# Two-layer trunk kernel: the second pair of heads projected between the first norms, side products spread anew, the gating norm by logarithm and exponential

## The reference

```python
h = rmsnorm(x, norm_mix_g[l]);  proj = h @ w_in[l]          # 1024 -> 5384 columns
logf = log_sigmoid(proj[F] + b_forget[l])                   # 8 forget gates
zc = gelu(proj[C]);  gates = sigmoid(proj[G] + b_gate[l])
y_a = pool_mixer(a, pool_w, pool_scale) @ w_branch_a        # means over 2, 4, 8, 16 positions
y_b = forgetting_attention(q, k, v, logf) @ w_branch_b      # 8 heads of 64, causal, bias F[t]-F[s]
y_c = spatial_gating(zc, sgu_norm_g, sgu_w, sgu_b) @ w_branch_c
x = x + (gates_a * y_a + gates_b * y_b + gates_c * y_c) @ w_out
# memory cross-attention: hx = rmsnorm(x), hm = rmsnorm(mem), 4 heads over 256 memory tokens
x = x + softmax(xq @ xk.T / 16) @ xv @ w_xo
x = x + square(relu(rmsnorm(x) @ w_ff1)) @ w_ff2
```

## Time and profile before

| | us |
|---|---|
| median of three timed runs | 2383.15 |
| profiled execution, its own time | 2365.17 |
| span of its slowest core (core 2) | 2363.5 |
| cores 0, 3, 6 | 2348.6, 2348.8, 2347.9 |
| cores 1, 4, 5, 7 | 2358.7, 2354.0, 2361.7, 2357.1 |
| TensorE busy, core 2 | 2276.2 |
| first scores of layer 0, core 2 | 79.03 |
| layer 1 begins | about 1202 |

### The profile page before, as it was taken

One profiled execution on the slowest core, in us unless ns is written; L12 is line 12 of the kernel. 1 busy time (PEld: TensorE's weight loads), 2 busy tenths in 40 slices (PEclk: granted clock), 3 DMA queues, 4 the chain that ended last, 5 costly groups with the idle time before them and its releaser, 6 DMA issues.

```text
span 2363.5 us, 37788 instructions; the slowest of 8 cores (2347.9 to 2363.5 us)
## 1 busy us (share of the span) xinstructions
PE 2276.2 (96%) x13762; PEld 1145.1 (48%) x13984; DVE 1158.9 (49%) x1829; ACT 955.8 (40%) x1460; POOL 283.7 (12%) x284
## 2 busy tenths in 40 slices
PE   5899999999999999999999999999999999999997
PEld 2465654444444444444456656444444444444444
DVE  3456544444546534344573665444444564334345
ACT  5577663323534212111357867332354430302023
POOL 5201310001102000000120031000011110000000
PEclk8899999999999999999999999999999999999999
DMA  7321572224502433331322029333252134332003
GB/s 179 60 29 20 93 132 37 36 37 76 82 13 35 57 43 36 36 45 37 91 80 30 11 44 136 66 50 47 47 90 36 19 48 51 39 43 27 1 37 108
DMA packets 170293, 128.87 MB, mean 55 GB/s; under 512 B 6912, under 2 KB 143488, under 8 KB 170112
## 3 DMA queue, kind: packets, MB, share of 16 engines
q0 software_dynamic: 139680, 80.92, 26.6%
q1 hardware_dynamic: 30432, 45.51, 6.5%
HBM read 190.14 MB, written 16.78 MB: 88 GB/s over the span
## 4 chain that ended last, share of the span: by engine, by line
PE 88%; issue 2%; DVE 2%; DMA 2%; POOL 2%; ACT 2%; SPq 0%; DVEq 0%; ACTq 0%; POOLq 0%
PE ps L490 88%; ACT pb L441 1%; POOL A L447 1%; DMA wide<-w_xo 1%; DMA x<-xT 1%; POOL sB L447 1%; SPq L477 0%; DMA wsl<-w_xkv 0%; DVE hm L454 0%; DVE x L454 0%; DVE T L454 0%; DVE kT L466 0%; DMA wsq<-w_qkv 0%; DVE dT L454 0%; POOL kT L474 0%
## 5 line engine op out<-in xcount | busy, mean ns | idle before, releaser
L490 PE MATMUL ps<-A,wsl 128*128 128x512 bf16 x3502 | 788.5, 379 | 5.8 <-DVE T L454 0.9
L490 PEld LDWEIGHTS ps<-A,wsl 128*128 128x128 bf16 x3584 | 348.3, 98 | 416.2 <-issue 2.2
L441 ACT ACTIVATE T<-ps 128x512 f32<-128x512 f32 x224 | 133.6, 596 | 587.3 <-PE ps L490 585.4
L447 DVE TENSOR_TENSOR x<-ps,x 128x512 f32<-128x512 f32 (+2 forms) x336 | 220.5, 665 | 302.0 <-PE ps L490 302.0
L490 PE MATMUL ps<-hid,wsl 128*128 128x512 bf16 x1506 | 330.9, 379 | 1.6
L441 ACT ACTIVATE pb<-ps 128x1024 bf16<-128x1024 f32 (+1 forms) x320 | 275.3, 895 | 57.8 <-PE ps L490 56.4
L490 PEld LDWEIGHTS ps<-hid,wsl 128*128 128x128 bf16 x1536 | 150.3, 98 | 181.2
L454 DVE SCALAR_TENSOR_TENSOR T<-T,ps 128x512 f32<-128x512 f32 x160 | 107.1, 686 | 261.6 <-PE ps L490 207.2
L447 DVE TENSOR_TENSOR hid<-T 128x512 bf16<-128x512 f32 x192 | 133.0, 693 | 206.0 <-ACT T L441 206.0
L441 ACT ACTIVATE T<-ps,halfb 128x512 f32<-128x512 f32 x128 | 88.0, 687 | 241.0 <-PE ps L490 238.2
L454 DVE SCALAR_TENSOR_TENSOR A<-x,vecs,rstd 128x512 bf16<-128x512 f32 x186 | 133.6, 785 | 26.0 <-ACT rstd L441 26.0
(11 more groups left out here) (140 smaller groups left out, 2396.9 us busy)
## 6 DMA issues: line engine op xcount, KB each, us to landing
wsl<-w_ff POOLq DMA_DIRECT2D x52, 512.0 KB, 6.9
x<-xT SPq DMA_DIRECT2D x64, 256.0 KB
wsl<-w_in POOLq DMA_DIRECT2D x30, 512.0 KB, 7.7
wsl<-w_xkv POOLq DMA_DIRECT2D x16, 512.0 KB, 8.2
xsave<-x SPq DMA_DIRECT2D x32, 256.0 KB
x<-xsave SPq DMA_DIRECT2D x32, 256.0 KB
wsq<-w_qkv POOLq DMA_DIRECT2D x24, 256.0 KB, 5.8
w<-w_ff POOLq DMA_DIRECT2D x12, 512.0 KB, 7.4
```

Of the source, the lines that this page charges most:

```text
L441: P.add("act", [lambda h: h.activation(out=o, in_=i_, func=func, scale=sc, bias=bi)], [out], [in_] + more, 175 + 0.833 * size(out) + 90 * ...
L447: P.add(eng, [lambda h: h.tensor_tensor(out=o, in0=a, in1=b, op=op)], [out], [in0, in1], cost)
L490: fns.append(lambda h, o=o, l_=l_, r_=r_, start=start, stop=stop, kw=kw: h.matmul(o, lhsT=l_, rhs=r_, start=start, stop=stop, **kw))
```

## The change

It has four parts.

1. The planner's landing time of a DMA can be given a slack: the four loads of `sgu_wT` are taken to land 15 us later, the eight of the memory input mT 60 us later. The DMAs themselves are unchanged.
2. Tiles 0 and 1 of pair 1 are projected ahead of the first attention, in between the norms and projections of pair 0, by a list of steps (n is a norm, i1 the initialization of pair 1's tiles, two digits the pair and the tile of a projection, f the forget gates). In layer 1, where x need not be loaded or normalized, the same list holds without the norms. So that pair 1's q, k and v can be written that early, they now lie over x's tile 0 and the start of tile 1, and the scratch of the forget gates moves out of that region.
3. The work laid between attention's steps is spread anew: pair 0 has tiles 2 and 3 of pair 1 and tiles 0 and 1 of pair 2; pair 1 has tiles 2 and 3 of pair 2, the gate path and five pieces of pooling; pair 2 begins with the gating norm and has the rest of pooling.
4. The gating norm is Exp(-0.5 Ln(...)) on ScalarE, in place of Sqrt and a reciprocal on VectorE.

```diff
-                done = max(bus + 1500, now + cost + 4000)
+                done = max(bus + 1500, now + cost + 4000) + op.lat
...
-            xr_ = Area(XR, 65536)
+            xr_ = Area(XR, 49152)
+            qT, kT, vz = [None, None], [None, None], [None, None]
+            qT[1] = [xr_.put("qT", [128, S], BF16) for i in range(2)]
+            kT[1] = [xr_.put("kT", [128, S], BF16) for i in range(2)]
+            vz[1] = xr_.put("vz", [128, 16, 2, 65], BF16)
             pb = [xr_.put("pb", [128, 2, 512], BF16) for i in range(3)]
...
-            E2t = [place("E2", [8, 512], F32, XR + 6144 + 2048 * i) for i in range(2)]
+            E2t = [place("E2", [8, 512], F32, MR + 2048 + 2048 * i) for i in range(2)]
...
-                        dma("sp", t_[:, 0:128].ap, sgu_wT[l, g], [t_[:, 0:128]], start_done, 65536)
+                        dma("sp", t_[:, 0:128].ap, sgu_wT[l, g], [t_[:, 0:128]], start_done, 65536, slack=15000)
...
-                    act(rs16[:, :], ss[:, :], AF.Sqrt, scale=1.0 / 256, bias=EPS)
-                    recip(rs16[:, :], rs16[:, :])
+                    act(rs16[:, :], ss[:, :], AF.Ln, scale=1.0 / 256, bias=EPS)
+                    act(rs16[:, :], rs16[:, :], AF.Exp, scale=-0.5)
...
-            for t in range(2):
-                if l == 0:
-                    norm_tile(lambda dc: xsl(dc, t), vb, lambda dc: Asl(dc, t), bank=bkn(), aside=(2, 5) if t else ())
-                for f in qkv(0, t, bk0):
-                    f()
-                forget(t, bkf)
-                qk_rows(0, t)
             pool_, (gate_v, gate_u) = pooling(), gating()
+            scale_v_ = gate_u.pop(9)
...
-            for f in norm0(2) + qkv(0, 2, bk0) + frow(2) + norm0(3) + qkv(0, 3, bk0) + frow(3):
-                f()
-            merge(at0, [lambda: qk_init(1)] + allqkv(1) + rows(1))
-            merge(attention(1), [lambda: qkv_w(1), lambda: qk_init(2)] + both(allqkv(2), gate_v) + rows(2))
+            begun = {"i1": [lambda: qk_init(1)]}
...
+            for what in "n0 n1 i1 00 f0 10 n2 01 f1 11 n3 02 f2 03 f3".split():
+                for f in begun[what]:
+                    f()
+            merge(at0, allqkv(1, 2) + rows(1) + [lambda: qkv_w(1), lambda: qk_init(2)] + allqkv(2, 0, 2))
+            merge(attention(1), both(allqkv(2, 2), gate_v + gate_u[:0] + pool_[:5]) + rows(2))
...
-                    dma("sp", mT[:, dc, :].ap, memT[dc], [mT[:, dc, :]], [], 131072)
+                    dma("sp", mT[:, dc, :].ap, memT[dc], [mT[:, dc, :]], [], 131072, slack=60000)
...
-            merge(attention(2), gate_u[:1] + [mem_norm] + both(allqkv(3), pool_) + rows(3))
+            merge(attention(2), gate_u[0:1] + [mem_norm, scale_v_] + both(allqkv(3), pool_[5:]) + rows(3))
```

More of the change, by code:

```diff
@@ L474, in memset, with dma @@
             P.add(eng, [lambda h: h.memset(a, val)], [v], [], 100 + size(v) / (0.96 if eng == "dve" else 1.1))
-        def dma(eng, out, in_, writes, reads, nbytes, group=None):
-            P.add(eng, [lambda h: h.dma_start(out=out, in_=in_)], writes, reads, 900 if eng == "pool" else 60, dma=True,
-                  group=group, nbytes=nbytes)
+        def dma(eng, out, in_, writes, reads, nbytes, group=None, slack=0):
+            P.add(eng, [lambda h: h.dma_start(out=out, in_=in_)], writes, reads, 900 if eng == "pool" else 60, lat=slack,
+                  dma=True, group=group, nbytes=nbytes)
         def mms(items, chunk=None):
@@ L621, in build @@
             vb = l * VPL
-            xr_ = Area(XR, 65536)
+            xr_ = Area(XR, 49152)
[3 more added lines that the diff above has]
+            vz[1] = xr_.put("vz", [128, 16, 2, 65], BF16)
             pb = [xr_.put("pb", [128, 2, 512], BF16) for i in range(3)]
-            qT = [[xr_.put("qT", [128, S], BF16) for i in range(2)] for s_ in range(2)]
-            kT = [[xr_.put("kT", [128, S], BF16) for i in range(2)] for s_ in range(2)]
-            vz = [xr_.put("vz", [128, 16, 2, 65], BF16) for s_ in range(2)]
+            qT[0] = [xr_.put("qT", [128, S], BF16) for i in range(2)]
+            kT[0] = [xr_.put("kT", [128, S], BF16) for i in range(2)]
+            vz[0] = xr_.put("vz", [128, 16, 2, 65], BF16)
             P3 = place("P3", [72, S], BF16, CR + 12288)
-            E2t = [place("E2", [8, 512], F32, XR + 6144 + 2048 * i) for i in range(2)]
-            tmpt = [place("tmpb", [8, 512], BF16, XR + 10240 + 1024 * i) for i in range(2)]
+            E2t = [place("E2", [8, 512], F32, MR + 2048 + 2048 * i) for i in range(2)]
+            tmpt = [place("tmpb", [8, 512], BF16, MR + 6144 + 1024 * i) for i in range(2)]
             et_rr = RR(list(zip(E2t, tmpt)))
-            run = place("run", [8, 1], F32, XR + 12288)
+            run = place("run", [8, 1], F32, MR + 8448)
             mr = Area(MR, 32768)
@@ L953, in build @@
             qk_init(0)
-            for t in range(2):
-                if l == 0:
-                    norm_tile(lambda dc: xsl(dc, t), vb, lambda dc: Asl(dc, t), bank=bkn(), aside=(2, 5) if t else ())
-                for f in qkv(0, t, bk0):
-                    f()
-                forget(t, bkf)
-                qk_rows(0, t)
             pool_, (gate_v, gate_u) = pooling(), gating()
+            scale_v_ = gate_u.pop(9)
             def norm0(t):
-                return [lambda: norm_tile(lambda dc: xsl(dc, t), vb, lambda dc: Asl(dc, t), bank=fb(), aside=(2, 5))] if l == 0 else []
+                return [lambda: norm_tile(lambda dc: xsl(dc, t), vb, lambda dc: Asl(dc, t), bank=fb(), aside=(2, 5) if t else ())] if l == 0 else []
             def both(a, c):
```

6 lines of the change are left out of this document (added).

## The result

| | before | after |
|---|---|---|
| median us | 2383.45 (2381.58 to 2384.99) | 2368.73 (2362.28 to 2368.73) |
| ratio of the comparison | | 0.9927, 95% interval 0.9913 to 0.9940 |
| profiled execution, its own time | 2365.17 | 2362.28 |
| slowest core of it | core 2, 2363.5 | core 1, 2360.7 |

What follows compares the result with a forecast made beforehand. TensorE, busy 96% of the span, was taken as the bound, with core 2 slowest. Savings of 9.5 + 6 + 1 - 1 = 15.5 us, with the 18 us to the timed runs kept, gave 2367.6 us, range 2357 to 2378.

Steps and rivals of the forecast that it cites:

- Part one: First attention scores: moving late squares of mT out of the first exponentials saves 9.5 us (8.7 to 10.8).
- the wait of 6.31 us: Core 2, after its first scores: TensorE's wait for an exponential goes, with 4.5 us of low clock behind it.
- Behind that, from 100 us to the end: After the first scores' stall on core 2, TensorE's remaining waits were taken to be small and scattered.
- What is late next: At the first scores, once the stall is gone: the next exponential, said to wait only for its scores.
- The check against core 3: First score to second block's transposition: core 3 takes 18.5 us, core 2 27.2; 8.7 us less.
- Part two: Prologue: projecting tiles 0 and 1 of the second pair there fills waits, net 6 us (0 to 8.8).
- the half clock at 45: Prologue, 45 to 50 us: 1.7 us of low clock, said to stay because the wait ahead of it stays.
- Part three: Gating norm: Ln and Exp save one ScalarE table load per layer, 1 us in all (0 to 2.6).
- Part four: Attention with 10.6 us less projections per layer: TensorE stays the bound, 1 us lost (2 gained to 21.2 lost).
- The sum: Whole kernel on core 2: 9.5 + 6 + 1 - 1 = 15.5 us saved, 2363.5 becomes 2348.
- The 18 us: Timed median of before, 2383.15, lies 18 us above its profiled execution; this distance was assumed unchanged.
- The marks: Signs to look for in the profile after: waits, clock, first score, nine table loads, attention's idle time, cores' spread.

Runs made afterwards that it cites:

- e1: The kernel before with only the eight mT loads counted 60 us later in the planner: 2361.2 us, ratio 0.9987.
- f4: The changed kernel as it is, measured again in a later comparison beside the kernel before: 2345.2 us, ratio 0.9923.
- g1: The kernel before with only pair 1's move into the prologue and its memory layout; no slack, pooling in pair 2, square root kept: 2360.3 us, ratio 0.9980.
- f3: The changed kernel with tiles 2 and 3 of pair 1 also projected in the prologue: 2363.4 us, ratio 1.0000.
- f2: The changed kernel with the five pieces of pooling put back into pair 2: 2359.1 us, ratio 0.9973.
- f1: The kernel before with late mT loads in the planner and five pieces of pooling moved from pair 2 to pair 1: 2360.5 us, ratio 0.9990.

## Why the prediction was right, and where not

**Part one, 9.5 us forecast, 3 to 4 measured.** This is the largest wrong term downwards: "the wait of 6.31 us goes, and so does the low clock behind it". Both went. But the run without them is only 3.1 us faster by the ratio and 3.6 by the mean core. I had measured a stall on the slowest core and priced the run with it; of eight cores five had the stall (2.95 to 6.65 us) and other cores had other ones, some behind the same first scores (E, on two cores of e1), some at 300 us (w_xkv, on five). "Behind that, from 100 us to the end, waits are small and scattered" missed the waits for w_xkv, up to 3.05 us on core 5 of before. "What is late next is the next exponential, which waits for nothing but its scores" was wrong: late next were E and w_xkv. The check against core 3 compared two cores up to 106 us and did not look at what came later.

**Part two, 6 forecast, 7.6 measured.** The weights were there, and the half clock at 45 stayed. The prologue's idle time fell by 5.5 us and its low clock by 2.1, which I had left out. That the first score of the slowest core came at 83.89 where 83.6 was forecast is luck. It follows x's arrival (in f4 the last squares that wait for a load of x stand at 37.1 to 45.9 us, the first scores at 74.0 to 81.6) and moves by several us from core to core: on core 2, for which the forecast was made, it stands at 79.03 in the profile before and at 74.49 in the one after. In the mean of the cores it went from 76.4 to 78.3, with 10.6 us more done ahead of it.

**Part three, 1 forecast, about 2 measured** (1.9 by the ratios, 0.7 of it seen as lost time in attention). Nine loads, as stated.

**Part four, -1 forecast, +4 to +7 measured.** The step that failed: "10.6 less filler in 254 us raises ScalarE's share by 4% ... I charge 1 us", and for the spread "2 us gained" at best. Thinning costs 4.7 us where pooling stays (g1) and 15 for the next 10.6 us (f3); the spread gains 11 to 12 (f2 against f4). Their sum is 7, and what the other parts leave of the whole 18.2 us is 4 to 6, since the parts do not simply add. ScalarE's share was read at the wrong place: the forecast had "some 34.5 of 40" for the changed kernel, whose busiest stretch has 36.9. And a load does not show what the spread won: waits for VectorE's on and for w_xkv. Of both I had no word.

**The sum** came out near by luck: part one was about 6 us too large, part four 5 to 8 and parts two and three together 2 to 3 too small. The chain g1 (-4.7), f2 (-6.4), f4 (-18.2) is what the runs put in its place: the last step, to which the forecast gave 2 us at its best end, is the largest.

**The 18 us** between the profiled execution and the median of before the forecast left as they were. The profile after, with up to 16 us of low clock in the MLP on die 0, suggests that the timed runs of before had the same and its profiled one had not. In the three later comparisons the medians of before lie within 1.3 us of its profiled 2365.17. Of its timed runs in the first comparison no clocks are known, so this is inferred, not shown.

**The marks.** No wait for pb above 1 us between first score and 100 us on any core: held (at most 0.32), with clock 1.00 there. Nine loads: held. TensorE's idle time in attention within 2 us of before: held in layer 1 (12.8 and 13.0), not in layer 0 (15.8 and 11.0, better). Waits for pb were not to grow by more than 5 us a layer: held (10.7 to 6.9 and 7.2 to 7.5). The stretch of layer 1's attention was to be no more than 10.6 us shorter; it is 11.5 (252.5 to 241.0), so this was missed by 1, but its prologue took up 12.0 (30.2 to 42.2), so layer 1 won nothing. The spread of the cores was to shrink to 6 us, and the forecast called itself wrong above 10: it is 28 us in the profile after and 9.9 in the mean of f4's five runs (12.3 before). That mark failed. What is left of the spread are the first scores, 74.0 to 81.6 on f4's cores, which follow x's arrival.

## What to carry to other kernels

A stall on the slowest of several cores is not the run's gain: list every wait above a microsecond on every core before pricing one, since the next core or the next stall sets the end when the first is gone. Price filler that is moved by the stretch in which the other engine is busiest (36.9 of 40 us here, where two stretches picked by hand had shown 33), and by the waits and the granted clock in windows of 5 us. Test a move and the new spread of what is left together: each was worth 5 us or less without the other (g1, f1), and the whole change, in which slack and norm make up 2 to 6 us, was worth 18. Where weights rotate through slots, look for the transfer with the shortest time between its issue and its use: 6 us between them stalled TensorE on most cores here, 10 us on none.

## What the runs showed of the hardware

The granted clock fell without any long wait ahead of it: in f2 on core 2 four waits (0.47, 0.81, 0.94 and 0.22 us, 2.4 in all) stand between 132 and 139 us, and the low clock lost 3 us more between 130 and 150 (0.78 and 0.88, a spell of 0.50 that begins at 135.5). The changed kernel, with a wait of 0.73 us at 129 and of at most 0.31 behind it, stayed at 1.00. No run changed these waits alone, so that they are the cause is likely and not shown. In the profile after, attention of layer 0 runs at clock 1.00 on seven of eight cores and takes 238.16 to 238.19 us on each of them (in f4 on six); before it took 249.5 to 261.5.

In the profile after, TensorE is busy without a gap in stretches of the MLP and still the cores of die 0 were granted less there (0.92 and 0.96 in the two windows shown) while core 6 had 1.00. In the four executions that the ratio counts the mean clocks were 0.983 to 0.990 on die 0 and 0.993 to 0.996 on die 1. What sets this off is open; f4, the same kernel, did not have it.

At the end of layer 1's attention TensorE sometimes stops for up to 3.7 us and the profile names no releaser. In the longest case the DMA engines are full (share 0.99). Core 6 of f1, the instruction behind the gap, then the window:

```profile
1474.24 0.43 PE L490 MATMUL ps<-vz,pb 128*128 128x65 bf16 x5 [3.69 <-issue]
```

```profile
1470.00:1475.00 5.00, 1.31 (x18) 0.88 0.99 148
```

Gaps of 0.9 us or more of this kind stood at this place in twelve of the fourteen profiles, on one to three cores, and in f1 on six. Their cause stays open; no run was made for it.
